# A decoder step with product-key experts: 96 prompt tokens instead of 32 sample tokens take their V rows by gather

## The reference

```python
q = (h @ wq).reshape(tokens, 8, 256)              # 8 heads
s1 = q[..., :128] . k1 ; s2 = q[..., 128:] . k2   # 128 keys each
v1, i1 = top_k(s1, 16); v2, i2 = top_k(s2, 16)
cand = v1[:, None] + v2[None, :]                  # 256 candidates
sc, sel = top_k(cand, 16)                         # 16 of 16384 experts, for each head
g = softmax(sc)
act = gelu(u[eidx] . h)                           # dot product with the row of U
out = sum over heads and picks of (g * act) * v[eidx]   # row of V
```

## Time and profile before

| what | value |
|---|---|
| median of 3 runs | 3559.99 us (3558.86 to 3561.13) |
| the profiled execution's own time | 3560.65 us |
| its span, first to last instruction | 3558.8 us |
| mean granted TensorE clock | 0.995 |
| PE busy | 3516.8 us (99%) |
| DVE busy | 2307.2 us (65%) |
| ACT busy | 1009.6 us (28%) |
| POOL busy | 186.7 us (5%) |
| DMA | 688.30 MB, mean 193 GB/s |

### The profile page before, as it was taken

One profiled execution on the slowest core, in us unless ns is written; L12 is line 12 of the kernel. 1 busy time (PEld: TensorE's weight loads), 2 busy tenths in 40 slices (PEclk: granted clock), 3 DMA queues, 4 the chain that ended last, 5 costly groups with the idle time before them and its releaser, 6 DMA issues.

```text
span 3558.8 us, 70400 instructions
## 1 busy us (share of the span) xinstructions
PE 3516.8 (99%) x31732; PEld 3017.9 (85%) x31732; DVE 2307.2 (65%) x3627; ACT 1009.6 (28%) x922; POOL 186.7 (5%) x160
## 2 busy tenths in 40 slices
PE   8999999999999999999999999999999999999998
PEld 5588888888888888888878888888888888888887
DVE  5979756555554677776555895556565466777765
ACT  4243333333342211121232433433333411111111
POOL 0000000000004101100000000000000050111000
PEclk9999999999999999999999999999999999999999
DMA  9921345555458556665323223646463775666541
GB/s 375 367 109 72 146 170 182 195 186 182 169 192 334 202 224 236 257 248 202 128 86 107 97 85 146 201 163 217 155 204 145 261 284 206 236 252 259 208 189 61
DMA packets 228719, 688.30 MB, mean 193 GB/s; under 512 B 14992, under 2 KB 152352, under 8 KB 193440
## 3 DMA queue, kind: packets, MB, share of 16 engines
q1 hardware_dynamic: 211824, 651.09, 49.1%
q0 software_dynamic: 11296, 33.60, 2.4%
q10 hardware_dynamic: 5392, 0.56, 0.1%
HBM read 539.92 MB, written 145.30 MB: 193 GB/s over the span
## 4 chain that ended last, share of the span: by engine, by line
PE 93%; DVE 3%; DMA 3%; ACT 1%; issue 0%; SPq 0%; DVEq 0%; ACTq 0%
PE PS L856 38%; PE PS L825 38%; PE PS L664 5%; PE PS L844 3%; PE PS L782 3%; PE PS L652 2%; PE PS L755 1%; PE PS L714 1%; DMA arena<-gates_dram 1%; DMA ring<-whole_w 1%; DVE ring L1488 1%; DMA arena<-act_dram 1%; PE PS L694 1%; PE PS L740 0%; ACT ring L1064 0%; PE PS L795 0%
## 5 line engine op out<-in xcount | busy, mean ns | idle before, releaser
L825 PE MATMUL PS<-X,ring 128*128 128x256 f16 (+1 forms) x12288 | 1435.3, 279 | 2.4 <-ACT arena L1260 2.4
L825 PEld LDWEIGHTS PS<-X,ring 128*128 128x128 f16 x12288 | 1199.4, 98 | 221.4 <-issue 2.8
L856 PE MATMUL PS<-arena,ring 128*128 128x256 f16 x12288 | 1345.4, 273 | 6.5 <-DVE ring L1488 6.5
L856 PEld LDWEIGHTS PS<-arena,ring 128*128 128x128 f16 x12288 | 1204.0, 98 | 147.7 <-issue 7.1
L1488 DVE SCALAR_TENSOR_TENSOR ring<-ring 128x4096 f16<-128x4096 f32 x148 | 654.5, 4423 | 540.0 <-ACT ring L1064 540.0
L1064 ACT ACTIVATE ring<-ring 128x4096 f16<-128x4096 f32 x148 | 535.1, 3616 | 1103.7 <-PE PS L856 1064.7
L1946 DVE TENSOR_TENSOR arena<-arena 128x512 f32<-128x512 f32 x256 | 279.4, 1092 | 438.1 <-PE PS L856 387.6
L1288 ACT ACTIVATE H<-PS 128x544 f32<-128x544 f32 x256 | 159.9, 625 | 979.0 <-PE PS L825 979.0
L1401 POOL DMA_INDIRECT ACC<-V,taps x64 | 89.7, 1402 | 2827.6 <-DMA gates_dram<-ACC 2143.2
L1950 DVE TENSOR_TENSOR arena<-arena 128x512 f16<-128x512 f32 x256 | 177.3, 693 | 8.8
L782 PE MATMUL PS<-X,ring 128*128 128x256 f16 (+1 forms) x1152 | 140.7, 283 | 4.0 <-DVE ring L1488 4.0
(11 more groups left out here) (205 smaller groups left out, 1853.7 us busy)
## 6 DMA issues: line engine op xcount, KB each, us to landing
ring<-U SPq DMA_DIRECT2D x64, 2048.0 KB, 10.6
ring<-V SPq DMA_DIRECT2D x64, 2048.0 KB, 7.9
act_dram<-H SPq DMA_DIRECT2D x64, 1088.0 KB, 5.0
gates_dram<-ACC SPq DMA_DIRECT2D x64, 1024.0 KB, 5.5
arena<-gates_dram SPq DMA_DIRECT2D x32, 2048.0 KB, 16.3
arena<-act_dram SPq DMA_DIRECT2D x64, 1024.0 KB, 12.1
ring<-split_w SPq DMA_DIRECT2D x17, 2048.0 KB, 8.6
arena<-whole_w SPq DMA_DIRECT2D x11, 2048.0 KB, 12.0
```

Of the source, the lines that this page charges most:

```text
L825: mm = pe.matmul(ps_row(u)[:, COLS[half]], parts[lane][:, pu, k * 512 + j * P:k * 512 + (j + 1) * P], h16(k, half, ph), start=(k == n == 0 ...
L856: mm = pe.matmul(ps_expert(i, h)[:, c % 2, :], parts[lane][:, pv, j * D + c * P:j * D + (c + 1) * P], WT[:, grp, pw, j, h * MID:(h + 1) * ...
```

## The change

The samples go the dense way now, and 96 tokens of the last prompt tile (tile 3, tokens 384 to 479) the sparse one. The dense way has 512 + 32 - 96 = 448 columns: 256 in the first half, 192 in the second. The other 32 tokens of tile 3 are columns 384 to 415, the samples 416 to 447.

`ROUTE` is now samples, tile 3, tiles 0, 1, 2, with spans of 4, 5, 7, 7, 7 groups. The samples and tile 3 have two batches each: 28 batches in all. The samples' picks are turned by 12 small matmuls, because they lie on four groups of head pairs.

The sparse part has `PICKS` = 128: one gather of V rows for each pick, 96 rows on 96 partitions, and one gather of activations. There are 8 row buffers (four in `ACC`, four in `H`), and VectorE takes picks in blocks of four (`own_block`), beginning in group 2 and ending in group 31; two groups have two blocks. GpSimd issues four activation gathers and four row gathers for each block, the rows each waiting for the sum that frees the buffer.

In the V phase VectorE does all four products first, then the raw slot's low half, then the four remainders (`weights_low`). The high halves of the products are made by ScalarE (`weights_high`), after the high half of the raw slot. Activations are loaded in two DMAs for each group (tokens 0 to 383 and 480 to 543). The sums are turned by eight matmuls of 96 columns (`own_to_columns`), and added by eight operations (`own_back`). `expert_pair` has three pieces for each chunk in the second half.

```diff
-ROUTE = (SAMPLE, 0, 1, 2, 3)
-SPAN = {SAMPLE: 2, 0: 7, 1: 7, 2: 7, 3: 7}
-PICKS = NS_ * HEADS * TOPK // P
-V_HOMES = 4
-SUMS_FROM, SUMS_BY = 8, 2
-TILE_BATCHES = {t: 0 if t == SAMPLE else P // BATCH for t in ROUTE}
+OWN_TILE = 3
+ROUTE = (SAMPLE, OWN_TILE, 0, 1, 2)
+SPAN = {SAMPLE: 4, OWN_TILE: 5, 0: 7, 1: 7, 2: 7}
+OWN = 96
+DENSE = T - OWN
+PICKS = HEADS * TOPK
+BLOCK = 4
+V_HOMES = 8
+TILE_BATCHES = {t: (NS_ if t == SAMPLE else P - OWN if t == OWN_TILE else P) // BATCH for t in ROUTE}
...
+                def load_act(lane, src):
+                    for at, to in ((0, OWN_AT), (OWN_SEG.stop, T)):
+                        n = to - at
+                        dst = 0 if at == 0 else OWN_AT
+                        sp.dma_start(AB[:, lane, :, dst:dst + n], src[:, :, at:to]).then_inc(act_in[lane], 16)
...
-                                           WT[:, grp, pw, j, h * MID:(h + 1) * MID],
+                                           WT[:, grp, pw, j, (0, MID)[h]:(MID, DENSE)[h]],
...
+                def weights_high(grp):
+                    for j in range(4):
+                        cast.n += 1
+                        act.wait_ge(wf_ready, cast.at())
+                        act.copy(WT[:, grp, 0, j, :], AB[:, grp, j, :]).then_inc(w_high, 1)
+                for grp in range(2):
+                    weights_high(grp)
+                with loop(act, BODIES - 1, (lanes[0], 1), (lanes[1], 1), (cast, 8)) as turn:
                     for lane in range(2):
                         act.wait_ge(v_done, turn * 2 + ((GROUPS - 1) * l + lane + 1))
                         high(lane, 1.0)
+                        weights_high(lane)
...
+                for i in range(V_HOMES // 2):
+                    gather_row(i)
                 for lane in range(2):
                     pool.wait_ge(act_stored[lane], 16 * (l + 1) * BODIES)
+                for i in range(2 * BLOCK):
+                    gather_act(i)
+                for i in range(V_HOMES // 2, V_HOMES):
+                    gather_row(i)
+                for n in range(2, PICKS // BLOCK):
+                    for i in range(BLOCK * n, BLOCK * (n + 1)):
+                        gather_act(i)
+                    for i in range(BLOCK * n, BLOCK * (n + 1)):
+                        gather_row(i)
...
+                def own_block(n):
+                    at = slice(BLOCK * n, BLOCK * (n + 1))
+                    dve.wait_ge(own_in[n % 4], 16 * BLOCK * (l * (PICKS // BLOCK // 4) + n // 4 + 1))
+                    link(dve.tensor_tensor(OWN_W[0:OWN, at], OWN_ACT[0:OWN, at], OWN_GATE[0:OWN, at], ALU.mult))
+                    for i in range(BLOCK * n, BLOCK * (n + 1)):
+                        own_sum(i)
...
+                def weights_low(group):
+                    grp = group % 2
+                    for j in range(4):
+                        wf.n += 1
+                        dve.wait_ge(w_high, wf.at())
+                        dve.tensor_tensor(WT[:, grp, 1, j, :], AB[:, grp, j, :], WT[:, grp, 0, j, :], ALU.subtract).then_inc(
+                            w_ready, 1)
...
                     if g > 1:
                         dve.wait_ge(v_done, (GROUPS - 1) * l + g - 1)
-                    for j in range(4):
-                        weigh(g, j)
+                    weigh(g)
                     low(g % 2, 1.0)
...
+                    weights_low(g)
+                    while block < (g - 1) * PICKS // (BLOCK * (GROUPS - 2)):
+                        own_block(block)
+                        block += 1
```

More of the change, by code:

```diff
@@ L150, in turn_group, with dense_at @@
 def turn_group(tile):
-    return None if tile == SAMPLE else SPAN[tile] - 3
+    if TILE_BATCHES[tile] == 0:
+        return None
+    return SPAN[tile] - (3 if TILE_BATCHES[tile] == P // BATCH else 2)
 def gate_steps(tile, i, j):
-    if tile == SAMPLE:
-        return range(0)
+    if TILE_BATCHES[tile] < P // BATCH:
+        return range(j, j + 1) if TILE_BATCHES[tile] and i == SPAN[tile] - 1 else range(0)
     first = i - (SPAN[tile] - 2)
     return range(8 * first + 2 * j, 8 * first + 2 * j + 2) if first >= 0 else range(0)
+def dense_at(tile, b):
+    if tile == SAMPLE:
+        return NP_ - OWN + b * BATCH
+    return tile * P + b * BATCH
 def _u_phase():
@@ L353, in build @@
         YS = early[:, 0:D]
[L354 to L359, removed]
+        v_home = [home[:, i * D:(i + 1) * D] for home in (ACCF, H[:, :, :].rearrange("p k t -> p (k t)"))
+                  for i in range(V_HOMES // 2)]
+        OWN_GATE, OWN_ACT, OWN_W = part(17408, PICKS), part(17536, PICKS), part(17664, PICKS)
+        ACT_I, ROW_I = part(17792, PICKS, dt=U32), part(17920, PICKS, dt=U32)
+        WHICH = spare_home[:, 0:1]
         S = part(0, 4, NQ, NKEYS)
@@ L438, in build @@
         v_done = sem("v_done")
[L439 removed]
+        rows_found, sums_done = (sem(x) for x in "rows_found sums_done".split())
+        own_in = [sem(f"own_in{i}") for i in range(4)]
         v_in = [sem(f"v_in{i}") for i in range(V_HOMES)]
@@ L833, in turn_picks @@
                 pe.wait_ge(gates_ready, n)
-                for j in range(2):
-                    pe.transpose(ps(u)[:, j * P:(j + 1) * P], KEYS[:, j, :], ident[:, :])
-                pe.transpose(ps(u)[:, 2 * P:3 * P], GG.rearrange("p h k -> p (h k)"), ident[:, :]).then_inc(mm_done, 1)
+                if sample:
+                    for g in range(4):
+                        at = g * NS_
+                        for j in range(2):
+                            pe.matmul(PS[at:at + NS_, place(u), j * P:j * P + NS_], KEYS[:, j, 0:NS_], ident[:, at:at + NS_],
+                                      start=True, stop=True)
+                        mm = pe.matmul(PS[at:at + NS_, place(u), 2 * P:2 * P + NS_], GG[:, 0:2, :].rearrange("p h k -> p (h k)"),
+                                       ident[:, at:at + NS_], start=True, stop=True)
+                else:
+                    for j in range(2):
+                        pe.transpose(ps(u)[:, j * P:(j + 1) * P], KEYS[:, j, :], ident[:, :])
+                    mm = pe.transpose(ps(u)[:, 2 * P:3 * P], GG.rearrange("p h k -> p (h k)"), ident[:, :])
+                mm.then_inc(mm_done, 1)
             def gate_step(buf, half):
```

162 lines of the change are left out of this document (79 added, 83 removed).

## The result

The changed kernel takes 3466.74 us in the median of four runs (3461.33 to 3469.12), the kernel before 3559.43 beside it (3552.38 to 3561.13): a ratio of 0.9741, 95% interval 0.9723 to 0.9759. The forecast of 3397 and its range (3380 to 3445) are both missed, on the slow side. The profiled execution took 3461.33 us, span 3459.5.

The account below looks back on a forecast made before the run. TensorE was taken as the bound, with 93% of the path that ends last. From 3560.65 us, -160.4 - 14.6 + 3 + 6 + 2 + 0.4 = -163.6 gave about 3397 us, with a range of 3380 to 3445 for 8 in 10.

Parts of the forecast that it names:

- ten openings a group: GpSimd in a V group: 8.53 gathers at 1.74 us, 14.9 of 18.5 us; running two blocks ahead was cover enough.
- is absorbed by 8: VectorE in the two groups with two blocks: weights ready at 10.5 us, needed at 18.5, so a 3.3 us lag is absorbed.
- Rival 1: V groups: GpSimd starved, TensorE waits for the sums; 2.85 us a gather, 3745 us, slower; chance 0.07.
- 192 columns: Second half of L856: 6144 matmuls go from 256 to 192 columns at 83.4 ns, gaining 160 us (0 to 181).
- Rival 3: Narrow L856 matmuls: the weight load of 98 ns is the floor, gain 71 us, 3487 us; chance 0.08, half at 89 ns.
- the estimate of 89 ns: Matmul spacing at 192 columns by a straight line between the skill's 81 and 131 ns; sum 36 us later, 3433.
- Gate steps and turned picks: TensorE: 16 gate steps less in both layers, 14.6 us gained; turning the samples' picks costs 1.5 us per layer, together 3.
- Start of V: TensorE idle before the V phase 5.7 us instead of 3.2, weights waiting for ScalarE's copies; 6 us lost in all (4 to 12).
- End of V: Returning 96 columns by 8 multiply-adds, 2.0 us where 0.8 was; with the expert pairs 2 us lost together (1 to 5).
- VectorE and ScalarE in a group: V group: VectorE 16.3 us (to 17.5) against TensorE's 18.5; ScalarE's copies under 2.6 us more, hidden in a steady group.
- Rival 2: VectorE becomes the bound of the V groups at 19.5 us instead of 16.3: 60 us lost, 3457 us; chance 0.10.
- Rival 4: DMA in V groups: at under 264 GB/s a group would be back at 21.2 us, against 303 forecast as hidden; chance 0.03.

Follow-up runs that it names:

- e1: Changed kernel with one block of sums in every group from 1 on, two only in the last: 3397.35 us, ratio 0.9548; one run of 3477.34 left out of the ratio.
- e2: Changed kernel with two waits of VectorE on its own results, ahead of the low half and behind it: 3396.97 us, ratio 0.9547.
- e4: Changed kernel with only 8 row gathers and 8 activation gathers a layer, all sums still made: 3395.51 us, ratio 0.9544.
- e3: Changed kernel with gates loaded for the first four groups only in each layer: 3462.27 us (3429.07 to 3470.39), ratio 0.9714.
- e7: Changed kernel with e1 and e2 together and ScalarE's casts of group 0 ahead of its last GELU: 3393.76 us (3385.86 to 3399.61), ratio 0.9542.
- e5: Changed kernel with one wait alone, VectorE waiting for its own last product ahead of the low half: 3394.83 us, ratio 0.9543.
- e6: Changed kernel with one wait alone, VectorE waiting for the low half before the remainders: 3394.44 us, ratio 0.9541.
- e8: e7 with all 128 tokens of the tile summed from gathered rows, second half 160 columns: 3289.39 us, ratio 0.9246.
- e10: e1 with the raw slot's low half computed twice by VectorE in groups 4 and 5 of each V phase: 3463.25 and 3540.08 us.

## Why the prediction was wrong

The step that failed is the one on GpSimd: "ten openings a group" at 1.74 us, with two blocks ahead as "cover enough"; and with it the sentence on VectorE that a lag "is absorbed by 8". Every end of an instruction was taken for an opening, whatever VectorE's schedule. On schedule the count holds: gathers take 1.58 us in the mean, and get in at the end of a low half with no wait behind it. When VectorE is 3 us late, the gather that is pending as the products begin is passed over at all ends of ten instructions, 10.2 us, and one gather takes 11.14 us. The lag of 3.3 us was computed, and held against TensorE's due time (8 us) alone; the gathers paid for it: the double block and one late group took their lead from 1.5 blocks to 0.3. The term of the sum that was put at nothing is the wait of the sums for rows: 139 us on VectorE, 65 us on the kernel. The rows before had it: the gather at 1122.24 took 5.21 us beside one instruction, but no row showed a gather held over several, and the rows' VectorE order had gaps that the change removed.

Rival 1 was this mechanism, with 0.07, and its threshold of 2.17 us a gather is borne out: that threshold counts from one gather to the next, and with the 0.30 between them the means are 1.88 us in the first 15 groups and 2.60 later. It was priced for all 60 groups at 2.85 us (3745), where it held in about half of them at 20.8 us a group, 2.60 us for each of 8 gathers. What was missing was a case between: right until a disturbance, then wrong for good.

The Trainium skill (SBUF — State Buffer, "Who interferes with whom") has a VectorE instruction with two SBUF inputs and a GpSimd one that reads SBUF exclude each other, the later one fully blocked until the first is done. The trace agrees for one instruction: the gather of 4.08 us that ends 0.77 after the low half. That a gather of 11.14 us was held over ten such instructions, and ended 0.73 us after them, is shown by the trace alone.

The other steps, each against its row:

- *192 columns*: forecast 83.4 ns. In e1, e2 and e4 the V phase of layer 0 takes 585.2 to 585.5 us; 6072 x (109.5 + 83.4)/2 is 585.7. The 83.9 of the 2880 matmuls is on the high side, because the slow start weighs more there. Rival 3 falls. So does the estimate of 89 ns, worked out from the spacings that the Trainium skill (TensorE: Matmul & The Clock Gate, "Back-to-back issue gap") states: the measurement decides.
- *Gate steps and turned picks*: 1792 matmuls in L876, as told. From the first matmul of the U phase to the first of the V phase layer 0 falls from 775.0 to 771.5 us and layer 1 from 775.1 to 772.1; forecast -7.3 + 1.5 + 3.0 = -2.8 each, measured -3.5 and -3.0.
- *Start of V*: a stop of 6.34 us, forecast 5.7, released by the remainders after ScalarE's cast, as told:

```profile
1106.96 3.62 ACT L1096 ACTIVATE ring<-ring 128x4096 f16<-128x4096 f32 x1 [0.73 <-DMA ring<-V]
1110.48 1.95 ACT L1371 CAST arena<-arena 128x448 f16<-128x448 f32 x4
1111.07 2.30 DVE L2017 TENSOR_TENSOR arena<-arena 128x448 f16<-128x448 f32 x4 [7.18 <-ACT arena L1371]
```

  The clock then stands at 0.50 for 4.1 us (window above); before it was 0.50 in the 2 us looked at the earlier trace rows.
- *End of V*: the eight multiply-adds of 96 columns take 1.89 us (L2044, at 1738.94), forecast 2.0.
- *VectorE and ScalarE in a group*: products 3.71, low half 4.43, remainders 2.23, weights 0.15, four sums 5.44: 16.0 us, forecast 16.3. The cast of 448 columns takes 0.56 us, and its wait is hidden. Rival 2 falls by e4.
- *DMA*: 307 GB/s in the good stretch, forecast 303, hidden at a share of 0.98. Rival 4 falls as the cause of this miss by e3 (a share of 0.83, and the stall) and e2 (1.00, and none); in e7 late loads did reach TensorE, for 9 us.

The sum was right but for the stall: without it the kernel runs in 3394 to 3397 us (e1, e2, e4, e5, e6), and 65 us of stall stand on top of it.

## What to carry to other kernels

Where one engine's issues get in only between another's instructions, look at which ends let them in, in that engine's late state as well as on schedule: an engine that is behind runs from one stage into the next without a wait, and here the gather pending at that seam was passed over for ten instructions. Where work is spread in uneven portions, ask what the largest portion does to every stock that the loop lives on (time ahead and transfers ahead), not to one of them; a loss that feeds itself begins at one group and lasts to the end. A single wait on the engine's own last result, 0.1 us a group, was worth 72 us here (e5, e6).

## What the runs showed of the hardware

- A gather's issue on GpSimd was held for 11.0 to 11.8 us by ten instructions of VectorE in a row when it was pending as they began (27 times in the changed kernel), and let in by a wait that left 0.03 to 0.1 us between two of them. Issued during a low half, it got in at that instruction's end without such a wait, 33 times of 33. Undisturbed it takes 0.91 us and 0.30 to the next.
- A DMA share of 1.00 at 307 GB/s (e2) went with no stall at all, and e8 moved 367 GB/s in the first 278 us of its V phase at 0.97. e7 stopped TensorE for late loads in layer 1 at 0.95 and 284 GB/s. The share alone didn't tell of a bound.
- The stall is not certain from one execution to the next: the profiled executions of e3 and e10 had it in one layer of two. The times suggest both layers for e10's 3540 and for e3's slower runs, and one for e1's 3477, but none of these was profiled.
